# Constant-tile products ahead of the first wait of five stages, and in the wait for the routing, of a two-block network kernel

## The chip, the cores and the metric

The kernel runs on one core of one Trainium2 chip. The metric is the device time of one execution in microseconds (us), as the median of several runs; less is better. The kernel before was timed in three runs: median 2951.44 us, 2947.84 to 2952.47.

## The reference

Two network blocks in float32, one after the other, over 512 tokens of width 1024 (528 with 16 meta tokens in the first):

```python
# first block
p = rmsnorm(h) @ w_in
y_a = s5_mixer(p[:, :o1])            # state space scan, then y * sigmoid(y @ w_glu)
y_b = hgrn2_mixer(p[:, o1:o5])       # chunked linear recurrence, 8 heads
h = h + (sigmoid(g1) * (y_a @ w_ssm_proj) + sigmoid(g2) * (y_b @ w_hgrn_proj)) @ w_out
h = h + (silu(u[:, :F]) * u[:, F:]) @ w_down      # u = causal_conv(rmsnorm(h) @ w_up)
# second block
p = rms_norm(x) @ w_in_2
merged = gated sum of (neighborhood attention, rwkv7 in both directions, memory attention)
x = x + merged @ w_out_2
# expert choice: 16 experts, each takes its 64 best tokens
affinity = softmax(h @ w_router)
top_val, top_idx = top_k(affinity.T, 64)
ye = (silu(xe @ w_gate[e]) * (xe @ w_up[e])) @ w_down[e] * top_val     # xe = h[top_idx]
x = x + scatter_add(ye);  return rms_norm(x)
```

## The kernel before

The program is a row of stages, each a block of its own: five instruction streams (SyncE, here SP, which mostly issues transfers; TensorE; ScalarE; VectorE; GpSimd) that are joined before the next stage begins. An engine runs its stream in the order written and stops at `wait_ge(semaphore, value)` until the value is reached. The stages in their order, with the prefix of their tiles: `in` (input projection), `s` (`s5_tail`), `hgrn` (`hgrn2`), `merge` (`project_chain`), `ffn`, `front`, `att` (`attentions`), `rw` (`rwkv7`), `merge_2`, and `moe` (`expert_ffn`).

Most large products are made in three passes over float32r halves (`three_passes`, lines 64 to 68): high times low, low times high, high times high. A product of plain float32 tiles is one call in the code and shows as two matmul records in the trace; a transpose is one record.

What each of the five stages waits for first on TensorE:
- `s5_tail`: the transfers of `u`, 32 of them, issued by SP (L1107) and ScalarE (L1171).
- `hgrn2`: the low half of the first weight tile, which VectorE makes (L1640).
- `project_chain`: the low half of its first weight tile, on VectorE (L253), after a load and a copy.
- `front`: the low half of the first weight tile, on VectorE (L2505).
- `attentions`: the query tile laid out by ScalarE (L2038), after loads.

The expert stage, `expert_ffn`, begins on TensorE with sums of the router's parts (L3494), then sixteen transposes of tokens (`turn_tokens(0..3)`, L3503). Then it waits for VectorE's affinities and transposes them (four transposes, L3511). VectorE needs that transpose to begin its search for each expert's 64 best tokens:

```python
split_low(0)
dve.wait_ge(aff_turned, 1)
step(nc.vector.tensor_copy(left, bank[0:EXPERTS, 1]))          # L3745
for r in range(CAPACITY // 8):
    step(nc.vector.max(best[:], left))                         # L3747
    step(nc.vector.match_replace(left, best[:], left, -1.0))   # L3748
    if r >= 1:
        split_low(r)                                           # L3740
```

`step` makes VectorE wait for its own instruction before the next. After the eight rounds, the places go to TensorE (L3517), back to VectorE, which writes the one-hot tiles (L3762), and TensorE gathers the tokens of four experts (L3532) and starts on the experts' weights (`hidden`, L3550; then L3578). The weights come through a ring of seven slots of 2 MB each, 192 loads issued by SP (L3485) in order; the eighth load waits until TensorE has done the first `hidden`, which frees two slots, and every later one waits likewise.

Of the kernel before, what the change touches and what calls it, by code (L numbers as in the profile page):

```python
# [70 lines left out]
def project_chain(nc, stage, steps, out_dram, x_raw, x_high, x_low, gain, gain_dram, sq_sum, w_next, w_next_high, w_next_low,  # L71
# [16 lines left out]
    with ExitStack() as ctx:  # L88
# [53 lines left out]
        with nc.Block() as block:  # L142
# [23 lines left out]
            def _(pe):  # L166
                for g, (n, j) in enumerate(slots):
# [417 lines left out]
def in_and_s5_weights(nc, stage, x_dram, gain_dram, w_dram, lam_dram, b_dram, c_dram, d_dram, eye_dram, ident_dram, ident,  # L585
# [6 lines left out]
    with ExitStack() as ctx:  # L592
# [51 lines left out]
        toep_zeroed = sem("toep_zeroed")  # L644
        toep_loaded = sem("toep_loaded")
# [19 lines left out]
        with nc.Block() as block:  # L665
# [24 lines left out]
            @block.gpsimd  # L690
            def _(pool):
                nc.gpsimd.memset(toep[:], 0.0).then_inc(toep_zeroed, 1)

# [373 lines left out]
def s5_tail(nc, stage, u_dram, ident, wbt, toep, ca, s_mag, table, out_dram):  # L1067
# [4 lines left out]
    with ExitStack() as ctx:  # L1072
# [28 lines left out]
        with nc.Block() as block:  # L1101
# [14 lines left out]
            def _(pe):  # L1116
                def inputs(m):
                    if m % 2 == 0:
                        pe.wait_ge(u_loaded[m // 2], 16 * CHUNK)
                    if m >= 2:  # L1120
                        pe.wait_ge(part_ready, 2 * (m - 1))
                    for i in range(4):
                        q = 4 * m + i
                        for r in (RE, IM):
                            for e in range(2):
                                last = nc.tensor.matmul(bank[64 * e:64 * e + 64, 2 * (m % 2) + r, i * COLS:(i + 1) * COLS],
                                                        wbt[:, q, r, 64 * e:64 * e + 64], u[:, 2 * q + e, :],
                                                        start=True, stop=True)
                    last.then_inc(input_made, 1)
# [109 lines left out]
def hgrn2(nc, stage, p_dram, lb_dram, gain_dram, ident_dram, mask_dram, out_dram, x_high, x_low, x_scale, w_dram, gates_dram):  # L1239
# [14 lines left out]
    with ExitStack() as ctx:  # L1254
# [112 lines left out]
        with nc.Block() as block:  # L1367
# [326 lines left out]
            def _(pe):  # L1694
                def turn(n):
# [121 lines left out]
def attentions(nc, stage, na_dram, mem_q_dram, mem_kv_dram, bias_dram, ident_dram, na_out_dram, mem_out_dram):  # L1817
# [11 lines left out]
    with ExitStack() as ctx:  # L1829
# [49 lines left out]
        with nc.Block() as block:  # L1879
# [20 lines left out]
            def _(pe):  # L1900
                def turn_values(j):
# [205 lines left out]
def front(nc, stage, h_dram, mem_dram, gains_dram, mem_gain_dram, w_dram, par_dram, mu_l_dram, lora_dram, ar, bh, kh, v, bonus,  # L2107
# [8 lines left out]
    with ExitStack() as ctx:  # L2116
# [123 lines left out]
        with nc.Block() as block:  # L2240
# [25 lines left out]
            def _(pe):  # L2266
                def products(n):
# [1107 lines left out]
def expert_ffn(nc, stage, acc, xg, router_parts, square_sums, select, ident, slots, gain, gate_dram, up_dram, down_dram, out_dram):  # L3375
# [13 lines left out]
    with ExitStack() as ctx:  # L3389
# [84 lines left out]
        with nc.Block() as block:  # L3474
# [17 lines left out]
            def _(pe):  # L3492
# [14 lines left out]
                for n in range(TT):  # L3507
                    turn_tokens(n)
                pe.wait_ge(route, MOE_AFFINITY)
# [322 lines left out]
def two_blocks(nc, d, out_dram):  # L3832
# [7 lines left out]
    p = scratch("p", 4 * D_MODEL + 2 * D_MODEL, LEN)  # L3840
    u = scratch("u", D_MODEL, LEN)
    ya_raw = scratch("ya_raw", D_MODEL, LEN)
    yb = scratch("yb", D_MODEL, LEN)
    h1 = scratch("h1", D_MODEL, LEN)
    h2 = scratch("h2", D_MODEL, LEN)
    with ExitStack() as keep:
        x_high = keep.enter_context(nc.sbuf_tensor("x_high", [P, KT, LEN], F32R))
        x_low = keep.enter_context(nc.sbuf_tensor("x_low", [P, KT, LEN], F32R))
        x_scale = keep.enter_context(nc.sbuf_tensor("x_scale", [P, 2, LEN // 2], F32))
        s5_only = ExitStack()  # L3850
        ident = s5_only.enter_context(nc.sbuf_tensor("s5_ident", [P, P], F32))
        wbt = s5_only.enter_context(nc.sbuf_tensor("s5_wbt", [P, PAIRS, 2, P], F32))
        toep = s5_only.enter_context(nc.sbuf_tensor("s5_toep", [P, 4, 2 * KT, CHUNK, SSM_GROUP], F32))
        ca = s5_only.enter_context(nc.sbuf_tensor("s5_ca", [P, 2, PAIRS, CHUNK + 1, SSM_GROUP], F32))
        s_mag = s5_only.enter_context(nc.sbuf_tensor("s5_mag", [P, PAIRS], F32))
        table = s5_only.enter_context(nc.sbuf_tensor("s5_table", [P, 2, PAIRS, COLS], F32))
        in_and_s5_weights(nc, "in", d["h"], d["mix_norm_g"], d["w_in"], d["ssm_lam"], d["ssm_b"], d["ssm_c"], d["ssm_d"],
                          d["ssm_eye"], d["ident"], ident, wbt, toep, ca, s_mag, table, x_high, x_low, x_scale, p, u)
        s5_tail(nc, "s5", u, ident, wbt, toep, ca, s_mag, table, ya_raw)
        s5_only.close()  # L3860
        hgrn2(nc, "hgrn", p[0:4 * D_MODEL], d["hgrn_lb"], d["hgrn_norm_g"], d["ident"], d["hgrn_mask"], yb, x_high, x_low, x_scale,
              d["w_in"][5 * D_MODEL:7 * D_MODEL], p[4 * D_MODEL:6 * D_MODEL])
    with ExitStack() as keep:
        x_high = keep.enter_context(nc.sbuf_tensor("ffn_x_high", [P, KT, LEN], F32R))
        x_low = keep.enter_context(nc.sbuf_tensor("ffn_x_low", [P, KT, LEN], F32R))
        sq_sum = keep.enter_context(nc.sbuf_tensor("ffn_sq_sum", [P, LEN], F32))
        gain = keep.enter_context(nc.sbuf_tensor("ffn_gain", [P, KT], F32))
        w = keep.enter_context(nc.sbuf_tensor("ffn_w", [P, 2, 2, KT, P], F32))
        place = -(-nc.sbuf_base // 32) * 32
        w_high = keep.enter_context(nc.sbuf_tensor("ffn_w_high", [P, 2, 2, KT, P], F32R))  # L3870
        w_low = keep.enter_context(nc.sbuf_tensor("ffn_w_low", [P, 2, 2, KT, P], F32R))
        x_raw = nc.alloc_sbuf_tensor_at("merge_x_raw", [P, KT, LEN], F32, offset=place)
        ff_tiles = D_FF // P
        first_weights = [d["w_up"][(g * ff_tiles + n) * P:(g * ff_tiles + n + 1) * P, :] for n in range(2) for g in range(2)]
        project_chain(nc, "merge", [(ya_raw, d["ssm_w_glu"], "glu", ya_raw, "x"),
                                    (None, d["w_ssm_proj"], "gate", p[4 * D_MODEL:5 * D_MODEL], "merged"),
                                    (yb, d["w_hgrn_proj"], "gate_add", p[5 * D_MODEL:6 * D_MODEL], "x"),
                                    (None, d["w_out"], "add", d["h"], "out")], h1, x_raw, x_high, x_low, gain, d["ffn_norm_g"], sq_sum,
                      w, w_high, w_low, first_weights)
        conv_gated_ffn(nc, "ffn", h1, x_high, x_low, sq_sum, w, w_high, w_low, d["w_up"], d["conv_w"], d["conv_b"], d["w_down"], h2)  # L3880


    x = scratch("x", D_MODEL, SEQ)
    widths = [3 * NA_WIDTH, MEM_WIDTH, 3 * D_MODEL]
    starts = [sum(widths[:n]) for n in range(len(widths) + 1)]
    p2 = scratch("p2", starts[-1], SEQ)
    p_na, q_mem, g_all = (p2[starts[n]:starts[n + 1]] for n in range(len(widths)))
    kv = scratch("kv", 2 * MEM_WIDTH, N_MEM)
    y_na = scratch("y_na", NA_WIDTH, SEQ)
    y_mem = scratch("y_mem", MEM_WIDTH, SEQ)  # L3890
    late = ExitStack()
    with late, ExitStack() as keep:
        def kept(name, *shape):
            return keep.enter_context(nc.sbuf_tensor(f"rw_{name}", [P, *shape], F32))

        operands = -(-nc.sbuf_base // 32) * 32
        ar = kept("ar", 2, RW_X, 2, SEQ)
        bh = kept("bh", 2, RW_X, SEQ)
        kh = kept("kh", 2, RW_X, SEQ)
        v = kept("v", 2, RW_X, SEQ)  # L3900
        bonus = kept("bonus", RW_X, SEQ)
        ends = kept("ends", RSTEPS, 2 * RW_X)
        lat_g = kept("lat_g", SEQ)
        front(nc, "front", h2[:, N_META:], d["mem"], d["gains_2"], d["norm_mem_g_2"], d["w_in_2"], d["rw_par"], d["rw_mu_l"],
              d["rw_lora"], ar, bh, kh, v, bonus, ends, lat_g, x, p2, kv)
        attentions(nc, "att", p_na, q_mem, kv, d["na_bias"], d["ident"], y_na, y_mem)
        x_bytes, w_bytes = 4 * KT * SEQ, 4 * 2 * D_MODEL
        x_high = nc.alloc_sbuf_tensor_at("merge_2_x_high", [P, KT, SEQ], F32R, offset=operands)
        x_low = nc.alloc_sbuf_tensor_at("merge_2_x_low", [P, KT, SEQ], F32R, offset=operands + x_bytes)
        w = nc.alloc_sbuf_tensor_at("merge_2_w", [P, 2, KT, P], F32, offset=operands + 2 * x_bytes)  # L3910
        w_high = nc.alloc_sbuf_tensor_at("merge_2_w_high", [P, 2, KT, P], F32R, offset=operands + 2 * x_bytes + w_bytes)
# [118 lines left out]
```

## Time and profile before

| | |
|---|---|
| median of three runs | 2951.44 us (2947.84 to 2952.47) |
| profiled execution, first to last instruction | 2951.6 us |
| TensorE busy | 2675.1 us, 91% of the span |
| VectorE busy | 1261.7 us, 43% |
| ScalarE busy | 800.0 us, 27% |
| HBM read, written | 568.84 MB, 38.99 MB |
| chain that ended last | DMA 21% of the span, TensorE 11%, VectorE 1% |

The profile is of one execution, and its span stands for its time: there is nothing around it that the profile shows. The mean clock granted to TensorE is 0.960 of full speed. Of full speed the rows show two levels, 1.00 (2.4 GHz) and 0.50 (1.2 GHz); a stretch with a number between holds a change from one to the other. The chain that ended last is followed back as far as the start of the expert stage, a third of the span; the stages ahead of it are read from the timeline.

### The profile page before, as it was taken

How to read it: one execution, taken by the hardware profiler on the slowest of the kernel's cores; microseconds unless marked ns; L12 is line 12 of the kernel's file. 1: busy time of each engine (PE TensorE's matmuls, PEld its weight loads, DVE VectorE, ACT ScalarE, POOL GpSimd, SP SyncE). 2: the span in 40 equal slices, each digit the busy share in tenths (PEclk: the TensorE clock that was granted, in tenths of full speed). 3: DMA queues.
4: the chain of work that ended last, by engine and by line, in shares of the span. 5: the costliest groups of instructions: out<-in, count | busy, mean ns of one | idle time of the engine just before them, and what ended most of it. 6: DMA issues, size and time to landing. Idle time of an engine off the chain costs nothing. (4 is left out here: it accounts for less than half of the span.)

```text
span 2951.6 us, 44568 instructions
## 1 busy us (share of the span) xinstructions
PE 2675.1 (91%) x18822; PEld 1940.4 (66%) x18822; DVE 1261.7 (43%) x2123; ACT 800.0 (27%) x1304; POOL 112.8 (4%) x90
## 2 busy tenths in 40 slices
PE   8997789799999998999889999879989899989887
PEld 8996677699999998778668888654333333333222
DVE  7764666444566632666363335751111111111112
ACT  3220454432434321543253332531000000000001
POOL 0000021000000000000002221000000000000000
PEclk9998899899999999999989999989999999999999
DMA  5447331455322233334420000548999999999996
GB/s 161 130 129 120 108 123 61 149 164 159 114 90 86 78 123 129 114 129 154 161 77 1 2 1 34 176 179 363 430 430 431 430 431 430 431 431 431 431 430 258
DMA packets 144437, 613.09 MB, mean 208 GB/s; under 512 B 37808, under 2 KB 57392, under 8 KB 119216
## 3 DMA queue, kind: packets, MB, share of 16 engines
q1 hardware_dynamic: 120576, 574.13, 50.7%
q10 hardware_dynamic: 23664, 36.11, 3.5%
q8 instruction: 151, 2.47, 0.3%
q14 instruction: 46, 0.38, 0.0%
HBM read 568.84 MB, written 38.99 MB: 206 GB/s over the span
## 5 line engine op out<-in xcount | busy, mean ns | idle before, releaser
L3550 PE MATMUL moe_bank<-moe_ring,xg 128*64 128x512 f32 x2048 | 494.1, 626 | 90.6 <-DMA moe_ring<-in_w_exp_up 89.3
L3550 PEld LDWEIGHTS moe_bank<-moe_ring,xg 128*64 128x64 f32 x2048 | 156.0, 142 | 370.9 <-issue 362.1
L3779 DVE TENSOR_TENSOR moe_sg<-moe_sg,moe_bank 64x512 f32<-64x512 f32 x64 | 44.1, 690 | 584.7 <-ACT moe_sg L3670 584.7
L3578 PE MATMUL moe_bank<-moe_ring,moe_act_t 128*64 128x512 f32 x1024 | 230.6, 592 | 0.5 <-ACT moe_act_t L3677 0.5
L66 PE MATMUL ffn_prod<-ffn_x_low,ffn_w_high 128*128 128x264 f32 x704 | 200.7, 285 | 5.9 <-PEq L142 5.9
L66 PE MATMUL in_bank<-x_low,in_w_high 128*128 128x264 f32 x640 | 187.3, 293 | 17.9 <-DVE in_w_low L982 9.2
L68 PE MATMUL ffn_prod<-ffn_x_high,ffn_w_high 128*128 128x264 f32 x704 | 200.9, 285 | 0.0
L67 PE MATMUL ffn_prod<-ffn_x_high,ffn_w_low 128*128 128x264 f32 x704 | 199.9, 284 | 0.0
L68 PE MATMUL in_bank<-x_high,in_w_high 128*128 128x264 f32 x640 | 184.6, 288 | 0.0
L67 PE MATMUL in_bank<-x_high,in_w_low 128*128 128x264 f32 x640 | 184.3, 288 | 0.0
L3578 PEld LDWEIGHTS moe_bank<-moe_ring,moe_act_t 128*64 128x64 f32 x1024 | 73.3, 137 | 146.3 <-issue 145.7
L3677 ACT COPY moe_act_t<-moe_bank 128x256 f32<-128x256 f32 x64 | 23.8, 372 | 515.7 <-PE moe_bank L3564 515.7
L66 PE MATMUL front_bank<-front_x_low,front_w_high 128*128 128x512 f32 x368 | 147.9, 402 | 11.8 <-DVE front_w_low L2505 11.7
L3787 DVE TENSOR_TENSOR acc<-acc,moe_bank 128x512 f32<-128x512 f32 x128 | 82.2, 684 | 174.2 <-PE moe_bank L3603 174.2
L67 PE MATMUL front_bank<-front_x_high,front_w_low 128*128 128x512 f32 x368 | 144.3, 392 | 0.0
L68 PE MATMUL front_bank<-front_x_high,front_w_high 128*128 128x512 f32 x368 | 144.1, 392 | 0.0
L66 PEld LDWEIGHTS ffn_prod<-ffn_x_low,ffn_w_high 128*128 128x128 f32 x704 | 133.1, 189 | 6.1 <-issue 6.1
L66 PEld LDWEIGHTS in_bank<-x_low,in_w_high 128*128 128x128 f32 x640 | 123.2, 192 | 19.6 <-issue 9.6
L67 PEld LDWEIGHTS ffn_prod<-ffn_x_high,ffn_w_low 128*128 128x128 f32 x704 | 133.2, 189 | 0.0
L68 PEld LDWEIGHTS ffn_prod<-ffn_x_high,ffn_w_high 128*128 128x128 f32 x704 | 133.0, 189 | 0.0
L67 PEld LDWEIGHTS in_bank<-x_high,in_w_low 128*128 128x128 f32 x640 | 123.8, 193 | 0.4 <-issue 0.2
L68 PEld LDWEIGHTS in_bank<-x_high,in_w_high 128*128 128x128 f32 x640 | 123.5, 193 | 0.0
(549 smaller groups left out, 5696.8 us busy)
## 6 DMA issues: line engine op xcount, KB each, us to landing
moe_ring<-in_w_exp_gate SPq DMA_DIRECT2D x64, 2048.0 KB, 27.7
moe_ring<-in_w_exp_up SPq DMA_DIRECT2D x64, 2048.0 KB, 21.3
moe_ring<-in_w_exp_down SPq DMA_DIRECT2D x64, 2048.0 KB, 25.9
front_w<-in_w_in SPq DMA_DIRECT2D x50, 512.0 KB, 3.6
ffn_w<-in_w_up SPq DMA_DIRECT2D x44, 512.0 KB, 4.4
in_w<-in_w_in SPq DMA_DIRECT2D x40, 512.0 KB, 4.1
ffn_w<-in_w_down SPq DMA_DIRECT2D x16, 704.0 KB, 4.0
p<-front_out ACTq DMA_DIRECT2D x35, 256.0 KB, 2.0
```

Of the source, the lines that this page charges most:

```text
L66: nc.tensor.matmul(to, w_high, x_low, start=start, stop=False)
L67: nc.tensor.matmul(to, w_low, x_high, start=False, stop=False)
L68: return nc.tensor.matmul(to, w_high, x_high, start=False, stop=stop)
L3550: last = nc.tensor.matmul(bank[64 * g:64 * g + 64, s], xe[:, (e // BATCH) % 2, k, at:at + CAPACITY], ring[:, slot_of(n, g), k * HALF:(k + ...
L3578: last = nc.tensor.matmul(bank[64 * h:64 * h + 64, 3 + e % 2], act_t[:, s, j], ring[:, slot, at:at + HALF], start=(c == 0 and j == 0), sto ...
L3677: nc.scalar.copy(act_t[:, s].rearrange("p j n -> p (j n)"), bank[:, 2, s * FT * CAPACITY:(s + 1) * FT * CAPACITY]).then_inc(act_t_ready, 1)
L3779: nc.vector.tensor_tensor(sg[0:CAPACITY, s], sg[0:CAPACITY, s], bank[64:64 + CAPACITY, s], ALU.mult).then_inc(act_ready, 1)
L3787: nc.vector.tensor_tensor(acc[:, FT * h + q], acc[:, FT * h + q], bank[:, part_bank(e, q) + h], ALU.add).then_inc(part_added, 1)
```

## The change

A tile `warm` of 128 x 128 float32 ones is kept in on-chip memory for the whole program. GpSimd fills it in the first stage, ahead of the zeroing of `toep`. Each call of the new function `keep_busy` multiplies it by itself a given number of times into a PSUM region that the stage's own work writes later; nobody reads the results, and they wait for nothing. 18 products stand at the head of TensorE's stream in `project_chain`, 8 in `s5_tail`, 10 in `hgrn2`, 20 in `attentions`, 12 in `front`, and 24 in `expert_ffn` behind the first sixteen token transposes. Everything else that the diff shows is the tile's allocation around the body, with its indentation, and the added argument.

```diff
+def keep_busy(nc, to, warm, count):
+
+    for _ in range(count):
+        nc.tensor.matmul(to, warm[:], warm[:], start=True, stop=True)
...
@@ project_chain, stream of TensorE
+                keep_busy(nc, y[:, 0, 0, 0, 0:P], warm, 18)
+
                 for g, (n, j) in enumerate(slots):
...
@@ in_and_s5_weights, stream of GpSimd
+                nc.gpsimd.memset(warm[:], 1.0).then_inc(warm_ready, 1)
                 nc.gpsimd.memset(toep[:], 0.0).then_inc(toep_zeroed, 1)
+                pool.wait_ge(warm_ready, 1)
...
@@ s5_tail, stream of TensorE
+                keep_busy(nc, bank[:, 0, 0:P], warm, 8)
...
@@ hgrn2, stream of TensorE
+                keep_busy(nc, bank[:, 0, 0:P], warm, 10)
...
@@ attentions, stream of TensorE
+                keep_busy(nc, bank[:, 0, 0:P], warm, 20)
...
@@ front, stream of TensorE
+                keep_busy(nc, bank[:, 0, 0:P], warm, 12)
...
@@ expert_ffn, stream of TensorE
                 for n in range(TT):
                     turn_tokens(n)
+                keep_busy(nc, bank[:, 7, 0:P], warm, 24)
                 pe.wait_ge(route, MOE_AFFINITY)
                 for t in range(TT):
                     last = nc.tensor.transpose(bank[0:EXPERTS, 1, t * P:(t + 1) * P], affinity[:, t], ident[:])
...
+    with nc.sbuf_tensor("warm", [P, P], F32) as warm:
```

## Rows read from the trace of the kernel before

**Rows 1.** The page: span of the profiled execution.

```profile
span 2951.6 us, 44568 instructions
```

**Rows 2.** Timeline of TensorE, start of the expert stage: start, duration in us, instruction, [idle before].

```profile
1967.21 1.04 PE L3494 MATMUL moe_bank<-select,router_parts 128*128 128x16 f32 x8 [0.52 <-PEq L3204]
...
1969.80 0.85 PE L3503 MATMUL moe_bank<-ident,xg 128*128 128x128 f32 x3
```

**Rows 3.** The chain that ended last, from the affinities to the gather: start, us, what.

```profile
1971.97 1.04 PE moe_bank L3511 x4
1973.03 0.69 DVE moe_sg L3745
...
1995.06 10.09 PE moe_bank L3532 x64
```

**Rows 4.** Timeline of TensorE in `rw`: float32 products of 128x128 by 128x128, two stretches.

```profile
1549.63 0.63 PE L2943 MATMUL rw_bank<-rw_z,rw_power 128*128 128x128 f32 x2
1550.06 0.63 PE L2941 MATMUL rw_bank<-rw_power 128*128 128x128 f32 x2
...
1604.77 0.39 PE L2942 MATMUL rw_bank<-rw_sm,rw_a_first 128*128 128x128 f32 x2
1604.99 0.39 PE L2943 MATMUL rw_bank<-rw_z,rw_sm 128*128 128x128 f32 x2
```

**Rows 5.** Windows; behind the engines' busy us: granted clock, DMA share, GB/s.

```profile
279.00:280.00 1.00, 0.00 (x0) 0.00 (x0) 0.16 (x2) 0.00 (x0) 0.00 (x0) 0.84 0.00 0
361.00:362.00 1.00, 1.00 (x8) 1.00 (x7) 0.04 (x1) 0.99 (x3) 0.00 (x0) 0.70 1.05 399
1167.00:1168.00 1.00, 0.00 (x0) 0.00 (x0) 0.00 (x0) 0.00 (x0) 0.00 (x0) 0.58 0.49 192
1180.00:1181.00 1.00, 1.00 (x4) 0.77 (x4) 1.00 (x3) 1.00 (x3) 0.00 (x0) 0.60 0.36 143
1549.00:1551.50 2.50, 2.50 (x12) 2.25 (x11) 0.00 (x0) 0.00 (x0) 0.00 (x0) 0.50 0.00 0
1969.00:1970.00 1.00, 1.00 (x8) 1.00 (x7) 0.00 (x0) 0.98 (x2) 0.00 (x0) 0.64 0.54 229
```

**Rows 6.** Timeline of SP's queue: the eighth load of expert weights.

```profile
2012.97 0.33 SPq L3485 DMA_DIRECT2D moe_ring<-in_w_exp_down  x1
```

**Rows 7.** Windows before and after that load, columns as in rows 5.

```profile
2003.50:2013.00 9.50, 8.78 (x48) 4.42 (x48) 0.00 (x0) 2.23 (x4) 0.00 (x0) 1.00 0.00 0
2013.00:2850.00 837.00, 755.02 (x3482) 272.05 (x3480) 130.34 (x196) 72.01 (x144) 0.00 (x0) 0.97 1.01 430
```

**Rows 8.** Timeline of SP's queue: the first transfer of each of the five stages.

```profile
279.76 0.35 SPq L1107 DMA_DIRECT2D s_u<-u  x1
...
351.92 0.33 SPq L1372 DMA_DIRECT2D hgrn_w<-in_w_in  x1
...
572.52 0.38 SPq L150 DMA_DIRECT2D merge_w<-in_ssm_w_glu  x1
...
1168.51 0.33 SPq L2244 DMA_DIRECT2D front_gains<-in_gains  x1
...
1464.58 0.38 SPq L1883 DMA_DIRECT2D att_v<-p  x1
```

**Rows 9.** Timeline of TensorE: the first product of each stage, and `hgrn`'s next wait.

```profile
286.17 0.38 PE L1126 MATMUL s_bank<-s_u,s_wbt 128*64 128x66 f32 x2 [9.69 <-DMA s_u<-u]
...
358.51 0.59 PE L66 MATMUL hgrn_bank<-x_low,hgrn_w_high 128*128 128x264 f32 x1 [10.26 <-DVE hgrn_w_low L1640]
...
368.55 0.45 PE L1702 MATMUL hgrn_bank<-hgrn_ident,hgrn_k_out 128*128 128x128 f32 x1 [2.55 <-POOL hgrn_k_out L1530]
...
583.47 0.59 PE L66 MATMUL merge_y<-ffn_x_low,merge_w_high 128*128 128x264 f32 x1 [13.66 <-DVE merge_w_low L253]
...
1175.74 0.80 PE L66 MATMUL front_bank<-front_x_low,front_w_high 128*128 128x512 f32 x1 [10.55 <-DVE front_w_low L2505]
...
1477.03 2.08 PE L1931 MATMUL att_bank<-att_k,att_q_laid 64*128 64x256 f32 x8 [15.06 <-ACT att_q_laid L2038]
```

More of the change, by code:

```diff
@@ L68, in three_passes, with project_chain @@
     return nc.tensor.matmul(to, w_high, x_high, start=False, stop=stop)
-def project_chain(nc, stage, steps, out_dram, x_raw, x_high, x_low, gain, gain_dram, sq_sum, w_next, w_next_high, w_next_low,
+def keep_busy(nc, to, warm, count):
+    for _ in range(count):
+        nc.tensor.matmul(to, warm[:], warm[:], start=True, stop=True)
+def project_chain(nc, warm, stage, steps, out_dram, x_raw, x_high, x_low, gain, gain_dram, sq_sum, w_next, w_next_high, w_next_low,
                   w_next_dram):
@@ L582, with in_and_s5_weights @@
 COLS = CHUNKS
-def in_and_s5_weights(nc, stage, x_dram, gain_dram, w_dram, lam_dram, b_dram, c_dram, d_dram, eye_dram, ident_dram, ident,
+def in_and_s5_weights(nc, warm, stage, x_dram, gain_dram, w_dram, lam_dram, b_dram, c_dram, d_dram, eye_dram, ident_dram, ident,
                       wbt, toep, ca, s_mag, table, x_high, x_low, scale, p_dram, u_dram):
@@ L644, in in_and_s5_weights @@
         toep_zeroed = sem("toep_zeroed")
+        warm_ready = sem("warm_ready")
         toep_loaded = sem("toep_loaded")
@@ L1064, with s5_tail @@
 S5_SLOT_TABLE = 29
-def s5_tail(nc, stage, u_dram, ident, wbt, toep, ca, s_mag, table, out_dram):
+def s5_tail(nc, warm, stage, u_dram, ident, wbt, toep, ca, s_mag, table, out_dram):
     GROUPS = 8
@@ L1236, with hgrn2 @@
 HCHUNKS = LEN // HCHUNK
-def hgrn2(nc, stage, p_dram, lb_dram, gain_dram, ident_dram, mask_dram, out_dram, x_high, x_low, x_scale, w_dram, gates_dram):
+def hgrn2(nc, warm, stage, p_dram, lb_dram, gain_dram, ident_dram, mask_dram, out_dram, x_high, x_low, x_scale, w_dram, gates_dram):
     SUPER = 2 * HCHUNK
@@ L1814, with attentions @@
 AHEAD = 3
-def attentions(nc, stage, na_dram, mem_q_dram, mem_kv_dram, bias_dram, ident_dram, na_out_dram, mem_out_dram):
+def attentions(nc, warm, stage, na_dram, mem_q_dram, mem_kv_dram, bias_dram, ident_dram, na_out_dram, mem_out_dram):
     T = SEQ
@@ L2104, with front @@
 FRONT_MEM = 33
-def front(nc, stage, h_dram, mem_dram, gains_dram, mem_gain_dram, w_dram, par_dram, mu_l_dram, lora_dram, ar, bh, kh, v, bonus,
+def front(nc, warm, stage, h_dram, mem_dram, gains_dram, mem_gain_dram, w_dram, par_dram, mu_l_dram, lora_dram, ar, bh, kh, v, bonus,
           ends, lat_g, x_dram, p_dram, kv_dram):
@@ L3372, with expert_ffn @@
 EXPERT_FF = 2 * D_MODEL
-def expert_ffn(nc, stage, acc, xg, router_parts, square_sums, select, ident, slots, gain, gate_dram, up_dram, down_dram, out_dram):
+def expert_ffn(nc, warm, stage, acc, xg, router_parts, square_sums, select, ident, slots, gain, gate_dram, up_dram, down_dram, out_dram):
     T = SEQ
@@ L3837, in scratch @@
         return nc.dram_tensor(name, (rows, cols), F32, kind="Internal").ap()
[L3840 to L3880, printed above, removed]
@@ L3883, in two_blocks @@
[L3883 to L3911, printed above, removed]
-        w_low = nc.alloc_sbuf_tensor_at("merge_2_w_low", [P, 2, KT, P], F32R, offset=operands + 2 * x_bytes + 2 * w_bytes)
-        rwkv7(nc, "rw", ar, bh, kh, v, bonus, ends, lat_g, d["rw_par"], d["rw_g2_2"], d["ident"], d["rw_masks"],
-              d["rw_member"], d["eye2"], (y_na, y_mem), d["w_merge_2"], x_high, x_low, w, w_high, w_low)
-        def kept_late(name, shape):
-            return late.enter_context(nc.sbuf_tensor(name, shape, F32, side="right"))
-        acc = kept_late("acc", [P, KT, SEQ])
-        xg = kept_late("xg", [P, KT, SEQ])
-        router_parts = kept_late("router_parts", [P, SEQ])
-        square_sums = kept_late("square_sums", [P, SEQ // P])
-        select = kept_late("select", [P, EXPERTS])
-        ident = kept_late("ident", [P, P])
-        slots = kept_late("slots", [P, CAPACITY])
-        gain = kept_late("final_gain", [P, KT])
-        constants = ((select[:], d["select"]), (ident[:], d["ident"]), (slots[:], d["slots"]), (gain[:], d["norm_final_g_2"]))
-        merge_and_router(nc, "merge_2", x_high, x_low, bonus, w, w_high, w_low, g_all, x, d["w_merge_2"], d["norm_ffn_g_2"],
-                         d["router_2"], constants, acc, xg, router_parts, square_sums)
-        keep.close()
-        expert_ffn(nc, "moe", acc, xg, router_parts, square_sums, select, ident, slots, gain, d["w_exp_gate_2"], d["w_exp_up_2"],
-                   d["w_exp_down_2"], out_dram)
```

88 lines of the change are left out of this document (added).

## The prediction

> **What bounds the kernel now.** I read the page first, then the chain of work that ended last, then timelines and windows around each place where the change adds work. The span is 2951.6 us [rows 1]; the median of the runs shown is 2951.44, so a sum made on the span needs no correction. Two things matter for this change. First, TensorE's clock. It is granted at half speed for a while after each idle stretch at the head of a stage, and returns to full speed some time after dense work has begun. Second, the expert stage, the last third of the span. From 2013 us on the DMA engines are busy throughout, at 430 GB/s [rows 7]: the experts' weights set the end. What comes before can only move the moment at which that stream gets going. It does have such a moment. For the 9.50 us before 2013.00 nothing moved at all [rows 7], because the ring of seven slots was full, and the eighth load was issued at 2012.97 [rows 6], when TensorE had done the first expert's first chunk. Behind that load the bytes still to come are fixed and their rate is fixed. So whatever delays TensorE on its way to that first chunk is added to the kernel in full, and whatever speeds it up is gained in full.
>
> The way to the first chunk is one chain without slack: the transpose of the affinities at 1971.97, the copy that starts VectorE's search at 1973.03, the search and the places, the gather at 1995.06 [rows 3], the first chunk. VectorE takes each step only when its last one is done, so the chain can't be squeezed.
>
> **The change, part by part.** The products are float32, 128x128 by 128x128. The `rw` stage has the same form: two records each, one product every 0.43 us (1549.63 to 1550.06) and every 0.22 us (1604.77 to 1604.99) [rows 4]; the former is at granted clock 0.50 [rows 5], and the latter I take as full clock, since records last 0.39 us there against 0.63. They wait for nothing, so they run from wherever TensorE's stream reaches them. TensorE enters a block at once: its first instruction in the expert stage came 0.52 us after the last of the stage before [rows 2]. So in the five stages I let them begin with SP's first transfer [rows 8].
>
> *The 24 products in the expert stage.* They don't stand in the long wait of the search, but ahead of the transpose that starts it. The last three transposes of tokens start at 1969.80, about 0.21 us apart (their 0.85 us over three and the tail of the last) [rows 2], so TensorE is free at 1969.80 + 3 x 0.21 = 1970.4. The affinities reach it at 1971.97 [rows 3]: there is room for 1.5 us of products. What 24 of them cost depends on the clock. It fell inside 1969 to 1970 (0.64 over that window, so at 1969.28) [rows 5], while the transposes ran. How long until it is back? After the first product of `hgrn` at 358.51 [rows 9] it rose at 361.60 (0.70 over 361 to 362 [rows 5]), 3.1 us later; after that of `front` at 1175.74 [rows 9] at 1180.80 (0.60 over 1180 to 1181 [rows 5]), 5.1 us later. The rises at the heads of the three other stages lie between.
> - Lowest: the clock comes back at once. 24 x 0.22 = 5.3 us, to 1975.7; the transpose of the affinities is 3.8 us late.
> - Rise 3.1 us after the first product: 3.1 / 0.43 = 7.2 products at half clock, 16.8 x 0.22 = 3.7 us for the rest, 6.8 us in all, to 1977.2: 5.3 us late.
> - Rise 5.1 us after it: 11.9 products, then 12.1 x 0.22 = 2.7, 7.8 us in all, to 1978.2: 6.2 us late.
> - Highest: half clock throughout, 24 x 0.43 = 10.3 us, to 1980.7: 8.7 us late.
>
> The transposes ahead of the products also count for something, or they don't: if they do, the rise may come before 3.1 us have passed. But the clock fell while they ran, so they can't be worth much. I take 5.5 us. Against it stands a small return: the four transposes of affinities took 1.04 us at half clock [rows 3], and would follow at full clock now, about 0.4 us shorter. The VectorE chain behind them is unchanged and lasts over 20 us, in which TensorE has only a few transposes to do, so the clock is down again at the gather as it was before: nothing is gained there. Net + 5.1 us, all of it on the chain. The only other work that runs there, the first seven loads, hides nothing: it ends by 2003.5 either way [rows 7] and then waits for this chain.
>
> The Trainium skill ("TensorE: Matmul & The Clock Gate", Part 4: PE-mode transpose) says that transposes don't bring the clock up, as they don't count as TensorE being busy in the same way. The row agrees so far as the clock fell during transposes; no row here has transposes alone for long enough to settle it. By that rule the rise is timed from the products alone, the lateness is the middle of 5.3 and 6.2, and the sum would be 0.3 us higher than mine.
>
> *The five stage heads.* What could be gained is the half-speed stretch ahead of the rise, which costs half its length: 3.1 / 2 = 1.5 us in `hgrn` to 5.1 / 2 = 2.5 us in `front`, the others between. For that the clock must be up at the end of the products and stay up until the first real product. It stayed up for 3.2 us after TensorE's last work ahead of `s` (286.17 - 9.69 = 276.48 [rows 9]; fall at 279.68, from 0.84 over 279 to 280 [rows 5]), and for 2.0 us ahead of `front` (1175.74 - 10.55 = 1165.19 [rows 9]; fall at 1167.16, from 0.58 [rows 5]). Now each stage, from its start [rows 8] and its first product [rows 9]:
> - `merge`: starts 572.52. 18 products with a rise after 3.1 to 5.1 us take 5.5 to 6.4 us, so they end by 579.0; 583.47 is 4.5 us off or more. The clock is down again. 0.
> - `att`: starts 1464.58. 20 products take 5.9 to 6.9 us, end by 1471.5; 1477.03 is 5.5 us off. 0.
> - `s`: starts 279.76. 8 products take 3.4 us at half clock and end at 283.2; the rise would have to come in that time and last the 3.0 us to 286.17. Both are at the edge: perhaps one time in six, for some 1 us.
> - `hgrn`: starts 351.92. 10 products end at 355.6 to 356.2, 2.3 to 2.9 us before 358.51. It may hold one time in three. But TensorE next stands still for 2.55 us until GpSimd's tile comes at 368.55 [rows 9], and 1.5 us earlier only lengthens that. 0.
> - `front`: starts 1168.51. 12 products end near 1173.3, 2.4 us before 1175.74. One time in three. At most 2.5 us; that stage's next weight tile is split behind all of the tokens' tiles, so I give it 1. Expected 0.3.
>
> In each stage the products end well ahead of the first real one (by 2.3 us at the least), so they cost nothing. If a stage's data came earlier than that, they would. Together - 0.3 us for the likeliest outcome. The fill of `warm` is one memset on GpSimd at the start, an engine on which nobody in that stage waits but for the zeroed `toep`, late in it: 0.
>
> **Sum.** 2951.6 + 5.5 - 0.4 - 0.3 = 2956.4 us, 0.17% above the median shown. That is inside 0.2% (5.9 us), about what a measurement of this kernel can tell from no change.
>
> **Rivals.**
> - *Slower by more than 0.2%.* The mechanism is the same, with the clock's rise late in the 24 products. It decides once the products' end is 6.3 us late or more with nothing from the stage heads, that is once they run past 1978.3: a rise more than about 5.2 us after their start, or none. For it: `front` needed 5.1 us. Against it: TensorE is dense from 1967.21 on [rows 2], so some of the wait for the rise may be served before the products begin. Up to 8.7 - 0.4 = + 8.3 us, 2959.9. Chance 0.34.
> - *The stage heads pay as well.* The clock holds over every gap. Four stages (`hgrn` is hidden) give 1.5 to 2.5 us each, 6 to 10; that against + 5.1 is 2947 to 2951. The falls after 2.0 and 3.2 us [rows 5, 9] speak against it for `merge` and `att`, whose gaps are 4.5 us and more; only `s` and `front` are open, 3.5 us together, 2953. Chance of 2 us or more: 0.10, nearly all of it inside 0.2%.
> - *The routing isn't on the path.* If the first chunk didn't wait for the search, or the weights' stream had slack, the 24 products would be hidden, and the kernel would be 0.3 to 3.5 us faster, 2948 to 2951. To be faster by over 0.2%, below 2945.5, both this and most of the stage heads must come true. Against it: 9.50 us without a transfer just ahead of the eighth load [rows 7]. Chance 0.05, a part of it for faster.
>
> The forecast itself, + 3 to + 5.9 us, has 0.51. Of the range: below stand the cases in which stage heads pay, above the late rise; 2952.5 to 2960.0 leaves out 2 in 10 at most. Chances: faster 0.03, same 0.63, slower 0.34.
>
> **What the profile of the changed kernel would show.** 48 records of the constant tile from about 1970.4 to 1977 or 1978; the transpose of the affinities right behind them with no wait of its own, at 1977 to 1978 instead of 1971.97; the gather and the eighth load later by the same 5 us; the stretch without a transfer grown from 10 to 15 us; 430 GB/s behind it as before. At the heads of `merge` and `att`, granted clock 0.50 at the first real product in spite of the products; in `front` and `hgrn` either. The prediction is wrong if the eighth load isn't later by what the affinities' transpose is, or if the products run at another pace than 0.43 and 0.22 us.

## The result, and the profile after

The changed kernel took 2957.56 us in the median of 20 runs (2951.44 to 2963.45), the kernel before 2951.11 us in 20 runs beside it (2945.82 to 2955.27). The ratio is 1.0024, 95% interval 1.0018 to 1.003: about 7 us slower. The forecast was 2956.4 in a range of 2952.5 to 2960.0, so the time is inside it; but of the three outcomes the measurement gives the one with a chance of 0.34, slower by over 0.2%, and only just: the interval begins at 1.0018.

The page of the profiled execution after. It is one of the shortest of the 20 (2952.54 us, for a span of 2950.5), so its span can't be set against that of [rows 1]; only stretches measured from their own stage's start can.

```profile
span 2950.5 us, 44938 instructions
...
PE 2699.3 (91%) x19006; PEld 1964.2 (67%) x19006; DVE 1261.6 (43%) x2123; ACT 799.3 (27%) x1304; POOL 112.8 (4%) x91
...
q8 instruction: 152, 2.49, 0.3%
```

There are 370 instructions more, four for each of the 92 products and two besides.

The timeline after: TensorE at the start of the expert stage, and SP's eighth load.

```profile
1962.24 1.04 PE L3513 MATMUL moe_bank<-select,router_parts 128*128 128x16 f32 x8 [0.52 <-PEq L3223]
1963.12 2.99 PE L3522 MATMUL moe_bank<-ident,xg 128*128 128x128 f32 x16
1965.91 6.17 PE L74 MATMUL moe_bank<-warm 128*128 128x128 f32 x48
1971.91 0.60 PE L3531 MATMUL moe_bank<-ident,moe_affinity 128*16 128x128 f32 x4
...
1994.58 9.39 PE L3552 MATMUL moe_bank<-moe_hot,moe_z_tok 128*128 128x256 f32 x64 [1.74 <-DVE moe_hot L3782]
...
2011.81 0.33 SPq L3504 DMA_DIRECT2D moe_ring<-in_w_exp_down  x1
```

Read it from the stage's first instruction. The affinities' transpose now comes 1971.91 - 1962.24 = 9.67 us behind it and waits for nothing; before it was 1971.97 - 1967.21 = 4.76 [rows 2, 3]. That is 4.9 us late. The transposes take 0.60 instead of 1.04, the gather 9.39 instead of 10.09 [rows 3]. The eighth load is 49.6 us behind the stage's start, before 45.8 [rows 2, 6]. In the eight profiles that have no products in this stage it lies between 44.9 and 45.8, so 0.9 us of it is spread between executions.

The windows after, around that load: TensorE's busy time, then the other engines', granted clock, DMA share, GB/s.

```profile
2001.00:2011.80 10.80, 10.08 (x59) 5.75 (x60) 0.00 (x0) 2.46 (x3) 0.00 (x0) 1.00 0.00 0
2011.80:2850.00 838.20, 754.80 (x3480) 270.72 (x3476) 130.30 (x196) 71.61 (x143) 0.00 (x0) 0.97 1.01 430
```

No transfer for at least 10.80 us, then 430 GB/s, as in [rows 7]. From the eighth load to the end it is 938.6 us before and 938.7 after (2950.5 - 2011.81). In all fourteen profiles of this study it lies between 938.5 and 939.1. So the whole tail hangs on that one load, one for one.

At the heads of the other stages the granted clock at the first real product is 0.50 in `s`, `hgrn`, `merge` and `att`, and 1.00 in `front`.

### The profile page after: what moved, and what is told of

Read it like the earlier page. It is cut to its first block and busy times, and to the rows that moved or that the text cites. A ratio compares the mean times of both kernels' runs of the same rounds, so it can differ in the third digit from the quotient of the medians.

```text
span 2950.5 us, 44938 instructions
## 1 busy us (share of the span) xinstructions
PE 2699.3 (91%) x19006; PEld 1964.2 (67%) x19006; DVE 1261.6 (43%) x2123; ACT 799.3 (27%) x1304; POOL 112.8 (4%) x91
```

## The experiments

Each kernel was timed beside the kernel before on one chip. Ratios are to it, with the 95% interval; the medians of the kernel before were 2951.75 (first four), 2951.06 (next four) and 2952.7 (last four). Diffs are against the changed kernel.

**The two halves, and the tile alone.**

```diff
 e1_routing_only: keep_busy(nc, bank[:, 7, 0:P], warm, 24) stays
-keep_busy(...) at the five stage heads
 e2_heads_only: the five heads stay
-keep_busy(nc, bank[:, 7, 0:P], warm, 24)
 e3_tile_only
-keep_busy(...) in all six places; the tile and its memset stay
```

> The tile and the 24 products ahead of the affinities' transpose; none at the five stage heads. Theory A (the routing products carry the whole loss, one for one): 5 us slower than before, ratio 1.0017, the affinities' transpose 9.7 us after the stage's start instead of 4.8, the eighth load of weights about 4 to 5 us later after the start than before (45.8). Theory B (the stage heads cost something as well, since all of the change together measured 6.5 us): 3 to 5 us here, the rest with the heads. Theory C (the tile's place in memory or the longer program costs): nearly as much here as in the kernel with the tile alone.

> The products at the five stage heads; none in the expert stage. Theory A: no measurable change, 0 to 1 us faster; granted clock 0.50 at the first real product of merge and att, either level in s, hgrn and front. Theory B: 1 to 3 us slower. The change's own aim (the clock is up at the first real product): 3 to 8 us faster.

> The tile is allocated and filled, no products anywhere. Theories A and B: the same as before, within 1.5 us. Theory C: 1.5 us slower or more.

Measured: e1 2956.55, 1.0016 (1.0007 to 1.0025), +4.8 us by medians. e2 2955.32, 1.0007 (0.9996 to 1.0019), +2 by the ratio, and by itself not told apart from nothing. e3 2952.44, 0.9997 (0.9988 to 1.0006). The tile alone costs nothing that the runs can tell, the products in the expert stage carry two thirds of the loss, and the heads seem to take something instead of giving it: e1 and e2 sum to 1.0023, against 1.0024 for both.

The timeline of e1, same places as above:

```profile
1966.80 1.86 PE L3508 MATMUL moe_bank<-select,router_parts 128*128 128x16 f32 x8 [0.52 <-PEq L3218]
...
1971.94 5.95 PE L74 MATMUL moe_bank<-warm 128*128 128x128 f32 x48
1977.72 0.60 PE L3526 MATMUL moe_bank<-ident,moe_affinity 128*16 128x128 f32 x4
...
2017.53 0.33 SPq L3499 DMA_DIRECT2D moe_ring<-in_w_exp_down  x1
```

The eighth load is 2017.53 - 1966.80 = 50.7 us behind the start, 5.0 later than before, with no head changed. The affinities' transpose is 1977.72 - 1966.80 = 10.9 us behind it, not the 9.7 that I expected, so 6.2 late: the clock was down until 1972.82 here, so the token transposes took longer and the products began 5.1 us behind the start, against 3.7 in the kernel after.

**A dose of the suspected wait: 48 products, and 6.**

```diff
 heads removed as in e1, and
-keep_busy(nc, bank[:, 7, 0:P], warm, 24)
+keep_busy(nc, bank[:, 7, 0:P], warm, 48)     # e4_routing_48; e8_routing_6 has 6
```

> As the routing kernel, with 48 products in place of 24 and none at the stage heads. Theory A (one for one, at full clock after the rise): the second 24 cost 24 x 0.22 = 5.3 us more, so 10 to 11 us slower than before, ratio 1.0036, and the eighth load later by the same. Rival (the weights' stream has slack): the second 24 cost less than half of that.

> 6 products instead of 24 ahead of the affinities' transpose, none elsewhere. Theory A (only what exceeds the 1.5 us of room is late): 6 x 0.43 = 2.6 us at half clock, 1.3 us at full; the affinities' transpose 4.8 to 5.9 us after the stage's start, the eighth load 45 to 47 us after it, the total within 1.2 us of before. Rival (each product costs its time): 1.3 to 2.6 us slower.

Measured: e4 2962.56, 1.0037 (1.0023 to 1.0051), +10.8; e8 2953.37, 1.0006 (0.9997 to 1.0015). The timeline of e4, whose first instruction of the stage starts at 1962.7:

```profile
1966.62 11.31 PE L74 MATMUL moe_bank<-warm 128*128 128x128 f32 x96
1977.77 0.60 PE L3526 MATMUL moe_bank<-ident,moe_affinity 128*16 128x128 f32 x4
...
2018.21 0.33 SPq L3499 DMA_DIRECT2D moe_ring<-in_w_exp_down  x1
```

The products fill 1977.77 - 1966.62 = 11.15 us, against 6.00 in the kernel after (1971.91 - 1965.91): the second 24 take 5.15 us, 0.215 each. The eighth load is 55.5 us behind the start, 9.7 later than before, and the time follows. The timeline of e8:

```profile
1964.67 1.20 PE L3508 MATMUL moe_bank<-select,router_parts 128*128 128x16 f32 x8 [0.52 <-PEq L3218]
1965.71 3.44 PE L3517 MATMUL moe_bank<-ident,xg 128*128 128x128 f32 x16
1968.99 1.50 PE L74 MATMUL moe_bank<-warm 128*128 128x128 f32 x12
1970.33 0.60 PE L3526 MATMUL moe_bank<-ident,moe_affinity 128*16 128x128 f32 x4
...
2010.12 0.33 SPq L3499 DMA_DIRECT2D moe_ring<-in_w_exp_down  x1
```

Six products fit nearly into the wait that was there: the transpose is 5.66 us behind the start (4.76 before), its four are shorter by 0.44, the gather (9.27) too, and the eighth load is 45.5 behind, as before. Nothing lost; the median's 2.3 us aren't told from zero.

**The products where the wait really is.** None ahead of the affinities' transpose; 28 in the search's wait, 4 in the one that follows.

```diff
 all six calls removed, and in expert_ffn
+keep_busy(nc, bank[:, 7, 0:P], warm, 28)
 pe.wait_ge(route, MOE_PLACES)
...
+keep_busy(nc, bank[:, 7, 0:P], warm, 4)
 pe.wait_ge(z_tok_ready, 2 * TT)
```

> No products at the stage heads and none ahead of the affinities' transpose; 28 in the wait for the places (9.8 us idle before) and 4 between the places' transpose and the gather (1.7 us idle). Theory A (the loss was the place of the 24 products, and everything between the expert stage's start and the eighth load passes to the end): the transpose of the affinities stays 4.8 us after the stage's start; the gather runs at full clock and takes 8 us instead of 10.1; the eighth load comes at 43.5 to 44 us after the start instead of 45.8; about 2 us faster than before. Rival (it doesn't matter where they stand): 4 us slower or more.

Measured: 2950.78, 1.0 (0.9991 to 1.0009). Its timeline (the stage's first instruction is at 1967.61):

```profile
1972.37 0.60 PE L3525 MATMUL moe_bank<-ident,moe_affinity 128*16 128x128 f32 x4 [1.93 <-DVE moe_affinity L3749]
...
1982.72 8.59 PE L74 MATMUL moe_bank<-warm 128*128 128x128 f32 x56
...
1993.05 1.16 PE L74 MATMUL moe_bank<-warm 128*128 128x128 f32 x8
...
1994.86 7.91 PE L3548 MATMUL moe_bank<-moe_hot,moe_z_tok 128*128 128x256 f32 x64 [0.65 <-DVE moe_hot L3778]
...
2010.60 0.33 SPq L3499 DMA_DIRECT2D moe_ring<-in_w_exp_down  x1
```

The transpose is back at 4.76 us behind the start, the gather takes 7.91 instead of 10.09 [rows 3], and the eighth load is at 43.0 instead of 45.8. The profile shows the 2 to 3 us gained (1.9 to 2.8 against the spread of 44.9 to 45.8); the timed runs can't confirm or deny a gain of 0.1%.

**The heads, made long enough to hold the clock.**

```diff
 no products in front and in the expert stage, and
-... warm, 8)  warm, 10)  warm, 18)  warm, 20)     # s, hgrn, merge, att
+... warm, 15) warm, 14)  warm, 34)  warm, 40)
```

> 15, 14, 34 and 40 products at the heads of s, hgrn, merge and att, so many that they reach near the first real product, none in front and none in the expert stage. Theory A (the heads were too short; a clock that is up at the first product pays half of the half-speed stretch where TensorE sets the pace): granted clock 1.00 at the first real product in merge and att, merge and ffn together 1 to 1.7 us shorter, att up to 1 us, hgrn unchanged since its next wait takes it, s up to 1 us; 2 to 4 us faster in total. Theory F for all of them (the next wait takes the head start everywhere): stage lengths as without products, total the same within 1.5 us.

Measured: 2949.32, 0.9996 (0.9987 to 1.0005). The clock stood at 1.00 at the first product of `s`, `hgrn` and `merge`; in `att` it fell 0.2 us into the real work (0.68 over 1476 to 1477, first product at 1476.20). Still the total doesn't tell a gain from nothing. One place shows why, the head of `merge`. The timeline of the kernel after there (SP's first load, the products, the copy and the first real product):

```profile
568.80 0.38 SPq L156 DMA_DIRECT2D merge_w<-in_ssm_w_glu  x1
...
576.88 1.90 ACT L200 CAST merge_w_high<-merge_w 128x2048 fp32r<-128x2048 f32 x1 [3.08 <-DMA merge_w<-in_ssm_w_glu]
...
581.16 0.59 PE L66 MATMUL merge_y<-ffn_x_low,merge_w_high 128*128 128x264 f32 x1 [5.31 <-DVE merge_w_low L261]
```

The timeline of e6, the same three:

```profile
569.71 0.38 SPq L156 DMA_DIRECT2D merge_w<-in_ssm_w_glu  x1
...
578.02 1.90 ACT L200 CAST merge_w_high<-merge_w 128x2048 fp32r<-128x2048 f32 x1 [2.26 <-DMA merge_w<-in_ssm_w_glu]
...
582.30 0.39 PE L66 MATMUL merge_y<-ffn_x_low,merge_w_high 128*128 128x264 f32 x1 [2.10 <-DVE merge_w_low L261]
```

The timeline of e3, which has no products, load and copy:

```profile
567.67 0.38 SPq L156 DMA_DIRECT2D merge_w<-in_ssm_w_glu  x1
...
574.26 1.90 ACT L199 CAST merge_w_high<-merge_w 128x2048 fp32r<-128x2048 f32 x1 [1.42 <-DMA merge_w<-in_ssm_w_glu]
```

From load to copy: 6.6 us in e3, 8.1 after, 8.3 in e6. The weight tile lands later, and TensorE's first product with it, 12.4 and 12.6 us behind the start instead of 11.0 [rows 8, 9]. What else moved there is in the DMA view of that head; of the kernel after (queue, packets, MB, share of the 16 engines):

```profile
q8 instruction: 1, 0.02, 0.5%
```

and of e6:

```profile
q8 instruction: 1, 0.02, 0.7%
```

One packet of the instruction queue, 16 KB, between 573 and 575 us after and before 571 in e6. Nearly all that this queue carries must be TensorE's, as 38,012 of the 44,938 instructions are matmuls and weight loads. The packet's 0.5% of 12.4 us on 16 engines is 1.0 us of one engine, inside the load. In e6 the products of `merge` did take 186.5 us from first to last instead of 188.1 before: the gain was made, and the later first product, by 1.6 us, took it.

The head of `s` says more, because e1, e3, e4, e5 and e7 to e12 have the same code up to its end, without products. In e4, e8 and e11 a packet came over 5 us ahead of the stage's first transfer and none between it and the first real product, which is 5.7, 5.7 and 6.0 us behind the start. In e1, e5, e9, e10 and e12 one came 1.0 to 1.5 us behind the start, and the first product at 6.0 to 6.7; in e3 and e7 it came at 1.7 and 1.9, and the first product at 7.6. The other four profiles fit in: 6.4 in the kernel before and e6 with a packet at 1.0, 7.3 after and 8.0 in e2 with one at 1.7 and 2.2. So with the same code the packet's place changes from one execution to the next, and the first product's goes with it. That one makes the other is likely, but not shown.

**Merge alone, with two lengths.**

```diff
 all other calls removed, and
-keep_busy(nc, y[:, 0, 0, 0, 0:P], warm, 18)
+keep_busy(nc, y[:, 0, 0, 0, 0:P], warm, 26)     # e9_merge_26; e10_merge_36 has 36
```

> Products at the head of merge alone, 26, which is 104 instructions. Theory I (a packet of 16 KB of instructions, which TensorE fetches because the products use up its instructions during the stage's first loads, delays the first weight tile by 1.2 to 1.6 us): from the changed kernel (72 to 144 instructions of products since the last stage without any) and the long heads (116 to 252) the fetch comes between 116 and 144 of them, so with 104 there is none; the first real product comes 10.8 to 11.0 us after the stage's start, as without products, at granted clock 1.00, and merge's products (first to last) take 186.5 us instead of 188; about 1.5 us faster than before. Rival (the products themselves disturb the loads or VectorE): the first real product comes 12.2 to 12.6 us after the start.

> The same with 36 products, 144 instructions. Theory I: one packet on the instruction queue in merge's head, the first real product 12.2 to 12.6 us after the start, at granted clock 1.00, products 186.5 us; no gain in total. If the products take longer than the wait they may be late by themselves: they end at 5.5 + (36 - 12.9) x 0.22 = 10.6 us after the start, before the first real one. Rival (no connection with the fetch): the same offset as with 26.

Measured: e9 2950.76, 0.9995 (0.9986 to 1.0005); e10 2946.54, 0.9981 (0.9973 to 0.999). The timeline of e10:

```profile
569.99 10.76 PE L74 MATMUL merge_y<-warm 128*128 128x128 f32 x72 [2.77 <-PEq L1379]
...
576.58 1.90 ACT L200 CAST merge_w_high<-merge_w 128x2048 fp32r<-128x2048 f32 x1 [1.41 <-DMA merge_w<-in_ssm_w_glu]
...
580.86 0.39 PE L66 MATMUL merge_y<-ffn_x_low,merge_w_high 128*128 128x264 f32 x1
```

Two more products than e6 has in `merge`, and the copy is again 6.6 us behind its load (SP's at 569.95). The instruction packet comes between 580.8 and 582, when the first tile has landed. So it isn't the products by themselves that slow the load. By its wording this is the rival's outcome, the same offset as with 26: I had expected the packet inside the head, and it came behind it. So e10 doesn't show what a packet does. The timeline of e9, the first product:

```profile
580.00 0.39 PE L66 MATMUL merge_y<-ffn_x_low,merge_w_high 128*128 128x264 f32 x1 [2.44 <-DVE merge_w_low L261]
```

The window of e9 one us behind it:

```profile
581.00:582.00 1.00, 1.00 (x7) 1.00 (x7) 1.00 (x3) 0.52 (x2) 0.00 (x0) 0.52 1.05 377
```

In e9 the clock was still 1.00 after 2.44 us of standing still, and fell at 581.0, a microsecond into the work: nothing gained, the stage's products take 188.1 us from first to last (187.8 to 189.1 in the kernels without a lasting clock). In e10, where the products run up to the first real one, it stays up, and they take 186.5. That is 1.5 to 2 us of the 5.6 that e10 gained.

**The search's wait and merge together.** e7's two calls and e9's.

> 26 products in merge's head, 28 in the wait for the places and 4 ahead of the gather, none elsewhere: the two places where TensorE's clock can be had for nothing. Sum of the parts: 1.5 us from merge, 2 to 2.8 us from the expert stage (eighth load 43.0 us after its start instead of 45.0 to 45.8), 3.5 to 4.3 us faster than before, ratio 0.9987. Rival (both are given back further on): the same as before within 1.5 us.

Measured: 2949.29, 0.9993 (0.9985 to 1.0002). The expert stage kept its gain (eighth load 44.1 behind the start), but `merge` began its work at 0.50, since the clock fell at 579.7 with the first product at 580.2. In both e9 and e11 the 26 products didn't carry the clock over the gap. How many would is not shown, as the fall doesn't come at a fixed distance: ahead of `front`, behind the same work, it came 2.0 to 5.3 us after TensorE's last instruction in the thirteen profiles other than e5.

**Front alone.**

```diff
 all other calls removed, and
 keep_busy(nc, bank[:, 0, 0:P], warm, 12)         # e5_front_only
+keep_busy(nc, bank[:, 0, 0:P], warm, 20)         # e12_front_20, in its place
```

> Only the 12 products at the head of front. Theory F (the head start is given back inside front, and then some): front lasts 2 to 3 us longer than without products (from its start to the start of att: about 298.9 against 296.1 to 296.9), TensorE waits again about 22 us after the stage's start for VectorE's low half of a weight tile, and the granted clock falls there once more; the total is 1 to 3 us slower. Rival (front's growth seen so far is chance, or comes from the other stages' products): front lasts 296 to 297 us and the total doesn't change.

> 20 products in front's head, none elsewhere, so that the clock is up at the first real product. Theory F2 (the head start is swallowed by VectorE's next weight tile 22 us after the start, and what front lost in the changed kernel came from a fetch of instructions at 1376 us and from the clock's fall at that wait): front lasts 296 to 298 us, TensorE waits 1.2 to 1.8 us for the low half of the weight tile 22 us after the start, no gain. Rival (a clock that is up pays here): front lasts 294 to 295 us.

Measured: e5 2953.76, 1.0009 (1.0 to 1.0018); e12 2958.15, 1.0016 (1.0006 to 1.0026). In e5 the clock was up while the 12 products ran, so they ended by 1168.3, 4.10 us ahead of the first real one at 1172.44, which ran at half clock. The experiment missed its condition, which is why e12 was run. In e12 the clock was up, and the kernel was slower: by 4.7 us by its ratio, of which its profile shows 1 to 1.7 in `front`. The timeline of the kernel after inside `front`:

```profile
1173.71 0.50 PE L66 MATMUL front_bank<-front_x_low,front_w_high 128*128 128x512 f32 x1 [1.76 <-DVE front_w_low L2524]
...
1188.58 0.50 PE L66 MATMUL front_bank<-front_x_low,front_w_high 128*128 128x512 f32 x1 [1.84 <-DVE front_w_low L2524]
```

The timeline of e12, the three waits behind its first product:

```profile
1180.03 0.50 PE L66 MATMUL front_bank<-front_x_low,front_w_high 128*128 128x512 f32 x1 [0.67 <-DVE front_x_low L2513]
1182.68 0.51 PE L66 MATMUL front_bank<-front_x_low,front_w_high 128*128 128x512 f32 x1 [0.29 <-DVE front_w_low L2520]
1190.26 0.50 PE L66 MATMUL front_bank<-front_x_low,front_w_high 128*128 128x512 f32 x1 [1.84 <-DVE front_w_low L2520]
```

TensorE starts at full speed and runs ahead of VectorE: it waits 0.67 + 0.29 + 1.84 = 2.80 us for tiles of it (0.55 + 0.45 + 1.84 after), where the kernel before waits 1.19 once, at 1190.48. That tile comes 22 us behind the stage's start in either, so what was gained is handed back. Then the clock falls. The windows of e12 at the fall and at the rise:

```profile
1191.00:1192.00 1.00, 1.00 (x4) 0.81 (x4) 0.90 (x2) 0.50 (x1) 0.00 (x0) 0.65 0.79 160
...
1194.00:1195.00 1.00, 1.00 (x5) 0.76 (x4) 0.90 (x2) 0.53 (x1) 0.00 (x0) 0.64 0.00 0
```

It is down from 1191.30 to 1194.72; in the kernel after from 1189.02 to 1192.42, in e2 from 1189.84 to 1193.26, and in none of the other eleven profiles. A wait of 1.84 us isn't enough for it, as e10 has the same one at that place without a fall. From the start of `front` to that of `att` it is 298.9 us after, 299.0 in e2 and 297.8 in e12, against 296.1 before and 296.2 to 296.8 in nine others. Nearly all of e12's 1.7 us more than before arise at the low stretch: TensorE's products are level with the kernel before ahead of it and 1.5 us late behind it. e10, with no fall, has 297.8 too, but there VectorE's tile came 23.5 us behind the start and not 22.

## Why the prediction was right, and where it wasn't

**The routing: right.** The affinities' transpose came 4.9 us late, for 5.5 predicted, with no wait of its own. The products needed 6.0 us for the 24, less than the 6.8 to 7.8 of the middle cases: the clock rose at 1967.25, 1.3 us behind the first of them, and at 1972.82 in e1, 0.9 behind, not 3.1 to 5.1. Against that they began 3.7 us behind the stage's start (5.1 in e1), not 3.2, as the transposes ahead ran at the low clock. The two misses partly cancel, which is luck in the 4.9. The pace of 0.215 and 0.43 us held. The return on the four transposes was the predicted 0.4. "Nothing is gained there" looks wrong for the gather, which is 0.7 shorter: the clock, down since 1977.49, rose at 1997.97, 3.4 us into it, while before it took to 2000.01, 4.9 us. But the gather takes 9.6 to 10.4 us in the eight profiles without products in the stage and 9.9 in e4, so a gain by the products isn't shown. Net + 3.8 us at the eighth load in the profile after, + 5.0 in e1, for + 5.1 predicted.

**Transposes and the clock.** The step behind those rises that failed is "the clock fell while they ran, so they can't be worth much". The windows of e8 at the transposes:

```profile
1967.00:1968.00 1.00, 1.00 (x7) 1.00 (x6) 0.42 (x2) 0.96 (x3) 0.00 (x0) 0.50 0.82 344
1968.00:1969.00 1.00, 1.00 (x8) 1.00 (x7) 0.53 (x4) 0.85 (x3) 0.00 (x0) 0.60 1.04 442
```

The clock of 0.60 puts the rise at 1968.8, and e8's products start at 1968.99. Between the fall at 1965.4 and that rise TensorE ran the last sums and sixteen transposes, and none of the tile's products. In e3, which has no products of the tile anywhere, it is the same. Its timeline:

```profile
1961.77 1.30 PE L3508 MATMUL moe_bank<-select,router_parts 128*128 128x16 f32 x8 [0.52 <-PEq L3218]
1962.91 3.34 PE L3517 MATMUL moe_bank<-ident,xg 128*128 128x128 f32 x16
```

Its windows at the fall and at the rise:

```profile
1962.00:1963.00 1.00, 1.00 (x9) 1.00 (x9) 0.65 (x3) 0.27 (x1) 0.00 (x0) 0.69 1.10 197
...
1965.00:1966.00 1.00, 1.00 (x8) 1.00 (x6) 0.57 (x3) 0.85 (x3) 0.00 (x0) 0.60 0.93 393
```

The clock fell at 1962.4 and rose at 1965.8, still among the transposes. So the wait for the rise was served while they ran, and the rival of a late rise failed as its own "against" had it. The Trainium skill ("TensorE: Matmul & The Clock Gate", Part 4: PE-mode transpose) has transposes not bring the clock up; for these float32 ones the trace disagrees, and the measurement decides.

**The tail: right.** 938.6 us behind the eighth load, whatever was ahead of it, and e4's + 9.7 us there is + 10.8 in the time.

**The stage heads: the term that was wrong.** It stood at - 0.3 and is about + 2: e2 has + 2 by its ratio, and the whole less e1 has 1.0024 - 1.0016, + 2.4. Neither alone is outside its uncertainty. The clock in the five heads was within what the prediction had, and the products did end ahead of the first real one (by 1.7 us at the least, in `hgrn`; 2.3 was predicted). The step that failed is "In each stage the products end well ahead of the first real one ..., so they cost nothing". It asked only whether they hold up TensorE, and left out two things. They lengthen the instruction stream, which moves its fetches, and in the profile after one fell into the first load of `merge`, whose first product came 1.4 us later (that the fetch caused it is argued, not shown). And in `front`, where the clock did hold, the "1" that it was given is no gain, since VectorE's tile is next, and a second low stretch of 3.4 us follows, 1.7 us of lost work. These two would make 3.1 us, more than the ratios give; a second instruction packet between 1376 and 1386 us stands beside another 1.1 us of idle time.

**The sum against the median.** "A sum made on the span needs no correction" was wrong by 1.9 us: in the runs of the kernel before the device time is 1.8 to 2.0 us above the span, in the changed one's 2.0 to 2.1 (2952.54 and 2950.5 in the profiled run). The profiled execution before stood therefore some 2.4 us above its median. Against the measured median the sum was 2951.1 + 4.8 = 2955.9 and 1.7 us short, which is the heads' term with a little of the routing's given back. So it was the heads' term, which the forecast had at nothing, that moved the result over 0.2%, and not the late rise that the rival gave for it. That 2956.4 lies only 1.2 us from the measured 2957.56 is partly luck, as its start was 0.5 us too high.

**What stays open.** The fetch was never moved alone by an edit; that it moves between executions of the same code, as in `s`, is the nearest to it. In all three profiles with a packet in the head of `merge` (after, e2, e6) the first product is 12.2 to 12.6 us behind the start, in all eleven without 10.7 to 11.0. Nor is it shown that the delay passes on to the end: from the start of `merge` to that of `front` it is 597.6 us after, against 595.7 to 597.5 in the eight profiles without products in `merge`. I expected e10's fetch elsewhere, so where one falls I can't foretell. Second, e10 is 5.6 us faster and its profile accounts for 2. Third, e5 has + 2.7 by its ratio and shows nothing in `front`, and e12 has + 4.7 and shows 1.7. Stages that no kernel changed differ between profiles by more than that (from the start of `rw` to that of the expert stage 426.1 us after, 430.7 before), and so do repeated runs of one kernel. Gains and losses of 2 us are therefore read from stretches here, and the totals only bound them.

## What to carry to other kernels

Warm-up products belong behind the last instruction that starts the long wait, never ahead of it: ahead, each delays the chain by its own length (24 cost 4 to 5 us, 24 more another 5), behind it 32 were free and shortened the next real work by 2.2 us, though the timed runs (ratio 1.0) don't show the gain. At a stage's head they must run until the first real product is ready, or nearly: 26 of them ended 2.4 us early and gave nothing, 36 in the same place gave 1.5 to 2. Each is one profile, and where the clock falls differs between executions by over 3 us. And ask what is next: where another engine's tile comes at a fixed moment, as in `front`, a faster start only lengthens the wait for it.

## What the runs showed of the hardware

- One 16 KB packet of the instruction queue in a stage's first load went with 1.0 to 1.7 us of delay of that load's tile (`merge` in three profiles; `hgrn` and `att` in e6, whose first product came 7.8 and 13.5 us behind the start, against 6.4 to 6.7 and 12.0 to 12.5). In `s`, where its place differs between executions, the first product came at 5.7 to 6.0 us with no packet in between and at 6.0 to 8.0 with one.
- Float32 transposes of 128x128 brought the clock back with no other product beside them: in e3 it fell at 1962.4 and rose at 1965.8, and TensorE ran 0.5 us of small sums and then only transposes in between.
- The distance from TensorE's last work to the fall of its clock isn't fixed: 2.0 to 5.3 us ahead of `front` in thirteen profiles.
- The clock can fall after the real work has begun again: in e9 it held through 2.44 us without work and fell 1.0 us into the next.
